# Sample state updates moved in front of the recurrent blocks, and score pages of every second group loaded into partitions 32 to 127

## The chip, the core and the metric

The kernel runs on one core of a Trainium2 chip. The metric is the device time of one execution in microseconds (us), the median of several runs. Engines are named as in the profile: PE (TensorE), DVE (VectorE), ACT (ScalarE), POOL (GpSimd) and SP (SyncE, which only issues transfers here). All engines run their own instruction streams and meet at semaphores.

## The reference, cut to what matters

One step of a two-layer model over a prompt of 512 tokens and, beside it, one new token for each of 8 samples. Everything is float32. Layer 0 has a mixer with two parts, and both occur twice, for the prompt and for the samples:

- an attention with a compressed cache. Each sample attends to 32 pages of 128 past tokens, gathered by a page table from HBM: scores with 8 heads, softmax, and the weighted sum of the values,
- a recurrence (`hgrn2`) with a 128x128 state for each of 4 heads. The prompt starts from zero and goes over 32 chunks of 16 tokens for each head. Each of the 8 samples makes one step from its stored state.

```python
qe = q * jnp.exp(bcum); ke = k * jnp.exp(-bcum); kd = k * jnp.exp(bcum[:, :, -1:] - bcum)
...
def step(S, xs):
    qe_c, kd_c, v_c, dec_c = xs
    o_c = jnp.einsum('btha,bhav->bthv', qe_c, S)
    S = dec_c[..., None] * S + jnp.einsum('btha,bthv->bhav', kd_c, v_c)
    return S, o_c
...
o = o * lax.rsqrt(jnp.mean(o * o, axis=-1, keepdims=True) + RMS_EPS) * g_out.astype(f32)
```

For a sample there is one token, so `S_new = f * S + k v` and `o = q S_new`, then the same norm. The rest of the layers are feed-forward blocks and projections, in which TensorE multiplies without a pause; the change doesn't touch them.

## The kernel before, in words

Everything is written out by hand: each engine has its own stream (`block.sync`, `block.gpsimd`, `block.scalar`, the vector and tensor streams), and in each the same stages follow one another: `ffn("ffn0")`, `ab_in()` (22 weight units), `queries()`, `hgrn()`, `keys()`, `prompts()`, `out_projection("ab_out")`, and the other layers. Weights come through three buffers `raw[0..2]` of 512 KB each, which SP loads in order; ACT and DVE split each into a high and a low part (`prefetch`, lines L250 and L256).

**The page work is spread over the stages by slots.** Numbered slots run from 0 up, and every engine calls `sample_to(end)` at the same places of its stream, which does the page work of all slots below `end`. The ends are set by `after_hgrn`, `after_state`, `after_norm`, `after_kv` and `after_prompt` (written out by hand: 4 slots to each of the 16 recurrent blocks, then 9 slots in the state part, 10 in the norm part, and so on). A *quad* is 4 jobs of 2 pages. Slots 3, 7, 11, ... each do the scores of one quad on PE (`scores`, L1685, 24 matmuls); 20 slots later the same quad's values are done (`values`, L1700); between them is the softmax of a sample, over slots 16 after its first.

Score pages go to `s_raw`, 8 slots for jobs, thus a ring of two quads: SP issues the 8 page loads of quad n+2 when the scores of quad n are done (`load_job`, L466). A score page is 96 partitions of 384 numbers (144 KB). Value pages (128 partitions, 128 KB) go to a ring `v_raw` of the same depth: POOL issues three of each four jobs (`pages_to`), SP the fourth, in between its score loads.

**`hgrn()`** has 16 blocks m (4 heads by 4 token blocks). For each, PE transposes and multiplies (`block_scores`), multiplies keys by values (`outer`, L1784), DVE goes over 8 chunk states one after the other in `s_ring` (L1282, L1285) and PE makes the outputs (L1808, L1814); ACT and DVE take them out of PSUM (L813, L1264). DVE's `sample_queries()` (L1145 to L1162), which lays out the samples' queries `q_s` and waits for the last of them, stands in front of block 0.

Behind block 15 comes **the state part**: k and v of the samples are transposed (L1823), copied (`ks_t` on ACT L821, `v_bd` on DVE L1304), multiplied in three sets (L1843), DVE makes the 32 updates of `st0` to `st7` (L1315), PE the outputs with `q_bd` (L1833), ACT the squares and the norm factors (L825 to L831: a square, `Ln`, `Exp`), DVE scales (L1322, L1325). POOL loads the states (L552): two of them near block 0, two behind block 15, four when the last square is done; it clears `q_bd` (L581) in between, and stores the new states (L589, L593). Then comes **the norm part** (scale, transpose back L1860, gate L1334, split into `m_hi` L838 and `m_lo`), and `keys()`.

Of the kernel before, what the change touches and what calls it, by code (L numbers as in the profile page):

```python
# [37 lines left out]
P = 128  # L38
D_MODEL, SEQ, BATCH_D, D_FF = 1024, 512, 8, 2816
NT = SEQ + BATCH_D  # L40
# [64 lines left out]
def build(nc, dram):  # L105
    ctx = ExitStack()
    with ctx:
# [58 lines left out]
        q_t, = tiles_at(R(0), ("q_t", [P, HEADS, NT]))  # L166
        v_raw = tiles_at(R(8), *[(f"v_raw{i}", [P, JOB, KV_LORA]) for i in range(RING)])
        w_uk, = tiles_at(R(8) + 4 * JOB * KV_LORA * 4, ("w_uk", [NOPE, HEADS, KV_LORA]))
# [4 lines left out]
        st4, st5, st6, st7 = tiles_at(R(28), *[(f"st{i}", [P, BH, P]) for i in range(4, BATCH_D)])  # L173
# [14 lines left out]
        def z_col(u):  # L188
            if u < C_F:
# [4 lines left out]
        kdv0, kdv1, kdv2, att0, att1, att2, v_blk0, v_blk1, s_ring, s_fin, st0, st1, self_row, q_s, own_k, o_lat, decay, p_own_c = tiles_at(  # L194
            work, *[(f"kdv{i}", [P, 2, P]) for i in range(3)], *[(f"att{i}", [P, P]) for i in range(3)],
            *[(f"v_blk{i}", [P, CH_ROW, P]) for i in range(2)], ("s_ring", [P, 2 * CH_BLK, P]), ("s_fin", [P, BH, P]),
            *[(f"st{i}", [P, BH, P]) for i in range(2)], ("self_row", [P, CC * P]), ("q_s", [P, BATCH_D, SK, CG]),
# [4 lines left out]
        st2, st3, v_bd, q_bd = tiles_at(at_blk, ("st2", [P, BH, P]), ("st3", [P, BH, P]), ("v_bd", [P, BATCH_D, P]),  # L202
                                        ("q_bd", [P, BH, BATCH_D * CG]))
        assert 2 * BH * P == 2 * CH_ROW * P and BATCH_D * P + BH * BATCH_D * CG == 2 * CH_BLK * P
        st = [st0, st1, st2, st3, st4, st5, st6, st7]
        kv_pad, ks_t, os_sb = tiles_at(work, ("kv_pad", [P, 2, BH, CG]), ("ks_t", [P, P]), ("os_sb", [P, P]))
# [205 lines left out]

        def after_hgrn(m, part):
            return 4 * m + part + 1

        def after_state(u):
            return 65 + u + 1

        def after_norm(n):
            return 73 + n + 1  # L420

# [30 lines left out]
        Q_S_STEPS = SK + 2  # L452
# [6 lines left out]
        def load_job(eng, kind, k, page_numbers):  # L459
            slots = s_raw if kind == "s" else v_raw  # L460
            if k >= RING:

                eng.wait_ge(S(f"{kind}_done"), k // COLG - RING // COLG + 1)
            rows, lo, width = (SR, 0, S_W) if kind == "s" else (PAGE, SR * S_W, KV_LORA)
            for j in range(JOB):
                eng.dma_start(slots[k % RING][0:rows, j, :],  # L466
                              dram["cache"][bass.ds(page_numbers[j], 1), lo:lo + rows * width].rearrange("a (p w) -> (a p) w", w=width)) \
                    .then_inc(loaded(kind, k), 16)

        def quad_loaded(eng, kind, q):  # L470

            uses = q // 2 + 1
            if kind == "s":
                eng.wait_ge(loaded("s", COLG * q), 16 * JOB * COLG * uses)
# [13 lines left out]
        def _(sp):  # L488
# [8 lines left out]

            sp.dma_start(gain[:], dram["gain"]).then_inc(S("gain_loaded"), 16)
# [39 lines left out]
        def _(pool):  # L538
# [42 lines left out]
            pool.memset(q_bd[:], 0.0).then_inc(S("q_cleared"), 1)  # L581
            pool.wait_ge(S("o_squared"), HG)
            for b in range(HALF_B, BATCH_D):
                state_in(b)
            pool.dma_start(dram["state_p"], s_fin[:]).then_inc(S("s_fin_stored"), 16)
            pages_to(after_state(3))
            pool.wait_ge(S("s_step"), BH * HALF_B)
            for b in range(HALF_B):
                pool.dma_start(dram["state_s"][b], st[b][:]).then_inc(S("st_stored"), 16)  # L589
            pages_to(after_state(7))  # L590
            pool.wait_ge(S("s_step"), BH * BATCH_D)
            for b in range(HALF_B, BATCH_D):
                pool.dma_start(dram["state_s"][b], st[b][:]).then_inc(S("st_stored"), 16)  # L593
# [15 lines left out]
        def _(act):  # L609
# [113 lines left out]
            def queries():  # L723
                n0, g0 = U0["uq"], G0["uq"]
                for h in range(HEADS):
# [12 lines left out]
                    if h in (2, 5, 7):  # L738
                        prefetch(n0 + (2, 5, 7).index(h))
# [46 lines left out]
            def hgrn():  # L786
# [14 lines left out]

                keep(0)
                keep(1)
                for m in range(HG):
# [6 lines left out]
                    sample_to(after_hgrn(m, 1))  # L811
                    act.wait_ge(S("o_mm"), m + 1)
# [5 lines left out]
                act.wait_ge(S("q_cleared"), 1)  # L818
                act.activation(q_bd[:, :, 0:BATCH_D * CG:CG + 1], z_q[:, :, SEQ:NT], ACT.Copy).then_inc(S("q_spread"), 1)
                act.wait_ge(S("kv_turned"), 1)  # L820
                act.activation(ks_t[:], bank[0][:, 0:P], ACT.Copy).then_inc(S("ks_kept"), 1)  # L821
                for u in range(-1, BATCH_D):
                    sample_to(after_state(u))
# [1262 lines left out]
```

## Time and profile before

| | us |
|---|---|
| median of 3 runs (lowest, highest) | 2275.16 (2272.53, 2280.35) |
| the profiled execution: its own time | 2284.63 |
| the profiled execution: its span | 2282.9 |
| PE busy, DVE busy, ACT busy (sum over the span) | 2185.3, 1036.6, 730.8 |
| recurrent blocks 0 to 15, on DVE | 556.95 to 680.34 |
| state part | 680.34 to 719.29 |
| norm part, then `keys()` and `prompts()` | 719.29 to 888.48 |

The last three rows are in us from the span's start. A group of instructions is read by its line number; a busy PE is not PE at its peak, since its matmuls overlap and the clock it is granted changes. The profiled execution is 9.5 us above the median of the runs shown, so differences are formed against its own time and carried over to the median.

### The profile page before, as it was taken

To read this page: it belongs to the slowest core of one execution; us is meant where nothing else is said; L and a number is where in the kernel's file an instruction comes from. 1 tells how busy PE (TensorE), PEld (TensorE's weight loads), DVE (VectorE), ACT (ScalarE), POOL (GpSimd) and SP (SyncE) were. 2 spreads that over 40 slices of the span, in tenths; PEclk is the share of its full clock that TensorE was granted. 3 is DMA by queue.
4 is the path that set the end of the run, shared out by engine and by line. 5 is a ranking of instruction groups with operands and counts; after the bars stand their busy time and mean duration, and the time that the engine had idled before them with its cause. 6 is when DMAs were issued, how large, how long until landed. Compare 5 with 4: busy or idle time off the path is not lost.

```text
span 2282.9 us, 46816 instructions
## 1 busy us (share of the span) xinstructions
PE 2185.3 (96%) x18285; PEld 2072.4 (91%) x18285; DVE 1036.6 (45%) x2002; ACT 730.8 (32%) x1292; POOL 120.2 (5%) x226
## 2 busy tenths in 40 slices
PE   8999999998776789999999999999999999999997
PEld 8999999997443458999999999999999999999997
DVE  5444434366654344544433444443446664444333
ACT  6222223354212333422222232222232233222222
POOL 0000000001234241000000000000000000000000
PEclk9999999998887789999999999999999999999999
DMA  4222223234799872222222222222322222222222
GB/s 162 92 92 92 92 102 100 81 125 147 213 265 279 236 212 93 84 92 92 92 92 100 97 91 91 92 92 92 102 92 92 92 93 92 88 87 91 94 100 75
DMA packets 101037, 261.98 MB, mean 115 GB/s; under 512 B 14385, under 2 KB 49218, under 8 KB 100866
## 3 DMA queue, kind: packets, MB, share of 16 engines
q1 hardware_dynamic: 89746, 228.83, 31.6%
q0 software_dynamic: 11184, 31.69, 4.7%
q8 instruction: 72, 1.18, 0.2%
q14 instruction: 35, 0.29, 0.0%
HBM read 255.29 MB, written 5.16 MB: 114 GB/s over the span
## 4 chain that ended last, share of the span: by engine, by line
PE 61%; DVE 1%; ACT 0%; issue 0%; DVEq 0%; ACTq 0%
PE bank L279 20%; PE bank L278 20%; PE bank L280 20%; PE bank L1929 1%; PE bank L1908 0%; PE bank L303 0%; DVE sb_x L1012 0%; PE bank L1921 0%; PE bank L1700 0%; PE bank L1943 0%; DVE sb_x L373 0%; ACT L312 0%; ACT sb_t L343 0%; DVE sb_h_lo L351 0%; ACT sb_h_hi L338 0%
## 5 line engine op out<-in xcount | busy, mean ns | idle before, releaser
L278 PE MATMUL bank<-sb_h_hi,sb_w_hi 128*128 128x260 f32 x3552 | 1005.9, 283 | 9.8 <-DVE sb_h_lo L1471 8.2
L279 PE MATMUL bank<-sb_h_lo,sb_w_hi 128*128 128x260 f32 x3552 | 1007.1, 284 | 0.0
L280 PE MATMUL bank<-sb_h_hi,sb_w_lo 128*128 128x260 f32 x3552 | 1003.8, 283 | 0.0
L250 ACT ACTIVATE sb_w_hi<-sb_raw 128x1024 fp32r<-128x1024 f32 x339 | 359.7, 1061 | 1260.8 <-PE bank L280 1257.1
L278 PEld LDWEIGHTS bank<-sb_h_hi,sb_w_hi 128*128 128x128 f32 x3552 | 668.5, 188 | 11.5 <-DVE sb_w_lo L256 8.3
L280 PEld LDWEIGHTS bank<-sb_h_hi,sb_w_lo 128*128 128x128 f32 x3552 | 671.4, 189 | 0.0
L279 PEld LDWEIGHTS bank<-sb_h_lo,sb_w_hi 128*128 128x128 f32 x3552 | 668.1, 188 | 0.2
L256 DVE TENSOR_TENSOR sb_w_lo<-sb_raw,sb_w_hi 128x1024 fp32r<-128x1024 f32 x339 | 415.3, 1225 | 382.4 <-ACT sb_w_hi L250 381.6
L279 PE MATMUL bank<-sb_a_lo,sb_w_hi 128*128 128x260 f32 x1408 | 399.1, 283 | 0.0
L278 PE MATMUL bank<-sb_a_hi,sb_w_hi 128*128 128x260 f32 x1408 | 398.7, 283 | 0.0
L280 PE MATMUL bank<-sb_a_hi,sb_w_lo 128*128 128x260 f32 x1408 | 397.7, 282 | 0.0
L280 PEld LDWEIGHTS bank<-sb_a_hi,sb_w_lo 128*128 128x128 f32 x1408 | 265.1, 188 | 0.0
L278 PEld LDWEIGHTS bank<-sb_a_hi,sb_w_hi 128*128 128x128 f32 x1408 | 264.9, 188 | 0.0
L279 PEld LDWEIGHTS bank<-sb_a_lo,sb_w_hi 128*128 128x128 f32 x1408 | 264.5, 188 | 0.0
L980 DVE TENSOR_TENSOR sb_t<-bank,sb_t 128x260 f32<-128x260 f32 x176 | 75.3, 429 | 261.1 <-PE bank L280 258.3
L972 DVE TENSOR_TENSOR sb_t<-bank,sb_r 128x260 f32<-128x260 f32 x176 | 74.4, 425 | 221.3 <-PE bank L280 200.7
L466 POOL DMA_DIRECT2D sb_v_raw<-in_cache x192 | 103.8, 541 | 195.0 <-PE bank L1700 176.2
L1685 PE MATMUL bank<-sb_s_raw,sb_q_s 96*32 96x256 f32 x768 | 60.1, 449 | 16.0 <-DMA sb_s_raw<-in_cache 8.8
L278 PE MATMUL bank<-sb_m_hi,sb_w_hi 128*128 128x260 f32 x256 | 73.2, 286 | 0.8 <-DVE sb_m_lo L1454 0.8
L279 PE MATMUL bank<-sb_m_lo,sb_w_hi 128*128 128x260 f32 x256 | 73.2, 286 | 0.0
L280 PE MATMUL bank<-sb_m_hi,sb_w_lo 128*128 128x260 f32 x256 | 73.0, 285 | 0.0
L985 DVE TENSOR_TENSOR sb_a_lo<-sb_t,sb_a_hi 128x260 f32 (+1 forms) x176 | 67.1, 423 | 0.0
(279 smaller groups left out, 1556.3 us busy)
## 6 DMA issues: line engine op xcount, KB each, us to landing
sb_raw<-in_w SPq DMA_DIRECT2D x339, 512.0 KB, 3.5
sb_s_raw<-in_cache SPq DMA_DIRECT2D x256, 144.0 KB, 4.7
sb_v_raw<-in_cache POOLq DMA_DIRECT2D x192, 128.0 KB, 5.3
sb_v_raw<-in_cache SPq DMA_DIRECT2D x64, 128.0 KB, 5.8
sb_x<-in_x SPq DMA_DIRECT2D x4, 520.0 KB, 6.2
out_y<-sb_x SPq DMA_DIRECT2D x8, 260.0 KB, 2.3
sb_st<-in_state POOLq DMA_DIRECT2D x8, 256.0 KB, 8.2
out_state_s<-sb_st POOLq DMA_DIRECT2D x8, 256.0 KB, 5.7
```

The lines of the kernel that those rows point to most:

```text
L250: nc.scalar.activation(w_hi[slot][:], raw[slot][:], ACT.Copy).then_inc(S("w_hi_done"), 1)
L256: nc.vector.tensor_tensor(w_lo[slot][:], raw[slot][:], w_hi[slot][:], ALU.subtract).then_inc(S("w_lo_done"), 1)
L278: nc.tensor.matmul(out, wh, xh, start=first and c == 0, stop=False)
L279: nc.tensor.matmul(out, wh, xl, start=False, stop=False)
L280: mm = nc.tensor.matmul(out, wl, xh, start=False, stop=last and c == chunks - 1)
L466: eng.dma_start(slots[k % RING][0:rows, j, :], dram["cache"][bass.ds(page_numbers[j], 1), lo:lo + rows * width].rearrange("a (p w) -> (a p ...
L972: dve.tensor_tensor(t1[:, half[hf]], pair(g, hf), r[:, half[hf]], ALU.mult) \
L980: dve.tensor_tensor(t3[:, half[hf]], pair(g + 1, hf), t2[:, half[hf]], ALU.mult) \
L985: dve.tensor_tensor(a_lo[:, ff, half[hf]], t3[:, half[hf]], a_hi[:, ff, half[hf]], ALU.subtract) \
L1685: last = mm(out, q_s[0:SR, i, c, :], s_raw[(COLG * n + j) % RING][0:SR, :, c * P:(c + 1) * P], start=q % 2 == 0 and c == 0, stop=q % 2 == ...
L1929: last = mm(bank[3][:, b * P:(b + 1) * P], v_t[:, k, vals], prob_t[:, tri(b) + k, :], start=k == 0, stop=k == b)
```

## The change

- The state part moves from behind block 15 to in front of block 0. The slots keep their order and number: `after_state(u)` is now `u + 2`, `after_hgrn` starts 9 later, the norm part's slots shift, and the slots of the norm part are handed out head by head.
- The samples' state outputs are normed on their own at the front (`norm_factors`, a `Ln` and an `Exp`), the prompt's 16 blocks behind block 15 (another `Ln` and `Exp`).
- All 8 states are loaded by POOL at once, when `ab_in()` is done. They now lie where the value ring `v_raw` lies, so POOL and SP start the value pages when the new states have been stored (`st_stored`).
- The parts of `sample_queries()` that need no queries (`own_rows`), and the padding of k and v (`state_rows`), go into `ab_in()`, units 20 and 21.
- The third of the weight splits of `queries()` goes to block 3. SP loads that stream's last weight unit before the pages (`n_cache - 1`) behind all pages instead.
- Score pages of odd quads: each page comes in two pieces, its rows 32 to 95 into partitions 32 to 95, and its rows 0 to 31 into partitions 96 to 127 (4 loads for each job instead of 2). POOL clears partitions 0 to 31 of these four slots once, `q_s` gets a copy of its rows 0 to 31 in rows 96 to 127, and the scores of odd quads contract over 128 rows instead of 96.

```diff
         q_t, = tiles_at(R(0), ("q_t", [P, HEADS, NT]))
+        st = tiles_at(R(8), *[(f"st{b}", [P, BH, P]) for b in range(BATCH_D)])
         v_raw = tiles_at(R(8), *[(f"v_raw{i}", [P, JOB, KV_LORA]) for i in range(RING)])
...
+        def after_state(u):
+            return u + 2
         def after_hgrn(m, part):
-            return 4 * m + part + 1
-        def after_state(u):
-            return 65 + u + 1
+            return 9 + 4 * m + part + 1
...
+            pieces = ((0, 0, rows),) if kind == "v" or k // COLG % 2 == 0 else ((LOW, LOW, SR - LOW), (SR, 0, LOW))
             for j in range(JOB):
-                eng.dma_start(slots[k % RING][0:rows, j, :],
-                              dram["cache"][bass.ds(page_numbers[j], 1), lo:lo + rows * width].rearrange("a (p w) -> (a p) w", w=width)) \
-                    .then_inc(loaded(kind, k), 16)
+                for to, row, count in pieces:
+                    first = lo + row * width
+                    eng.dma_start(slots[k % RING][to:to + count, j, :],
+                                  dram["cache"][bass.ds(page_numbers[j], 1), first:first + count * width].rearrange("a (p w) -> (a p) w", w=width)) \
+                        .then_inc(loaded(kind, k), 16)
...
-            stream(n_mid, n_cache)
+            stream(n_mid, n_cache - 3)
+            load(n_cache - 3)
+            load(n_cache - 2)
...
-                    if k - LAG == RING - 1:
-                        sp.wait_ge(S("q_lat_mm"), 1)
+                    if k - LAG == COLG - 1:
+                        sp.wait_ge(S("st_stored"), 16 * BATCH_D)
                     load_job(sp, "v", k - LAG, page_numbers(sp, k - LAG, 1)[0])
+            load(n_cache - 1)
```

POOL's stream, from the load of `w_uk` on:

```diff
-            pages_to(LAG - 4)
-            pool.wait_ge(S("ckv_stored"), 16)
-            pool.wait_ge(S("q_s_ready"), Q_S_STEPS)
-            state_in(0)
-            state_in(1)
+            for b in range(BATCH_D):
+                state_in(b)
+            pool.wait_ge(S("half_done"), 2 * U0["ukv"])
+            for i in range(COLG, RING):
+                pool.memset(s_raw[i][0:LOW], 0.0).then_inc(S("s_cleared"), 1)
             pool.wait_ge(S("q_lat_mm"), 1)
+            pool.memset(q_bd[:], 0.0).then_inc(S("q_cleared"), 1)
+            pool.wait_ge(S("s_step"), BH * HALF_B)
+            for b in range(HALF_B):
+                pool.dma_start(dram["state_s"][b], st[b][:]).then_inc(S("st_stored"), 16)
+            pool.wait_ge(S("s_step"), BH * BATCH_D)
+            pool.wait_ge(S("os_mm"), 1)
+            for b in range(HALF_B, BATCH_D):
+                pool.dma_start(dram["state_s"][b], st[b][:]).then_inc(S("st_stored"), 16)
+            pool.wait_ge(S("st_stored"), 16 * BATCH_D)
             for m in range(HG):
                 pages_to(after_hgrn(m, 3))
             pool.wait_ge(S("final_kept"), BH)
-            pool.wait_ge(S("o_mm"), HG)
-            state_in(2)
-            state_in(3)
-            pool.memset(q_bd[:], 0.0).then_inc(S("q_cleared"), 1)
-            pool.wait_ge(S("o_squared"), HG)
...
             pool.dma_start(dram["state_p"], s_fin[:]).then_inc(S("s_fin_stored"), 16)
```

DVE's `hgrn()` (the loop of the updates, lines L1307 to L1318, moves as it is), and what goes from `sample_queries()` into `ab_in()`:

```diff
+                    if u == 20:
+                        own_rows()
+                    if u == 21:
+                        state_rows()
...
+                dve.wait_ge(S("kv_turned"), 1)
+                dve.tensor_copy(vs_t[:], V_BANK[:, 0:P]).then_inc(S("vs_kept"), 1)
+                sample_queries()
+                dve.wait_ge(S("q_lat_mm"), 1)
+                dve.wait_ge(S("vs_kept"), 1)
+                dve.tensor_tensor(v_bd[:], vs_t[:].unsqueeze(1).to_broadcast([P, BATCH_D, P]),
+                                  cst[:, C_DIAG:C_DIAG + BATCH_D].unsqueeze(2).to_broadcast([P, BATCH_D, P]), ALU.mult).then_inc(S("v_spread"), 1)
...
                 masked(0)
                 masked(1)
-                sample_queries()
+                dve.wait_ge(S("o_factor"), 1)
+                dve.tensor_scalar(os_sb[:], os_sb[:], o_fac[:, HG:HG + 1], None, ALU.mult).then_inc(S("o_scaled"), 1)
+                dve.wait_ge(S("o_turned_back"), 1)
...
+                dve.tensor_copy(q_s[SR:P, :, :, 0:HEADS], q_s[0:LOW, :, :, 0:HEADS]).then_inc(S("q_s_ready"), 1)
```

ACT's `hgrn()`, and PE's scores:

```diff
                 keep(0)
                 keep(1)
+                act.wait_ge(S("os_kept"), 1)
+                act.activation(os_sq[:], os_sb[:], ACT.Square, accum_out=o_ss[:, HG:HG + 1]).then_inc(S("os_squared"), 1)
+                act.wait_ge(S("os_squared"), 1)
+                norm_factors(slice(HG, HG + 1), 1)
                 for m in range(HG):
...
+                    if m == 3:
+                        prefetch(U0["uq"] + UQ_UNITS - 1)
...
                 squared(HG - 1)
+                act.wait_ge(S("o_squared"), HG)
+                norm_factors(slice(0, HG), 2)
...
-                        last = mm(out, q_s[0:SR, i, c, :], s_raw[(COLG * n + j) % RING][0:SR, :, c * P:(c + 1) * P],
+                        last = mm(out, q_s[rows, i, c, :], s_raw[(COLG * n + j) % RING][rows, :, c * P:(c + 1) * P],
```

## Rows read from the trace of the kernel before

**Rows 1.** The page: the span, and the issues of the state loads (KB each, us to landing)

```profile
span 2282.9 us, 46816 instructions
...
sb_st<-in_state POOLq DMA_DIRECT2D x8, 256.0 KB, 8.2
```

**Rows 2.** Windows by stage: length, busy of PE, PEld, DVE, ACT, POOL, clock, DMA share, GB/s

```profile
556.95:581.35 24.40, 19.51 (x204) 10.16 (x204) 16.28 (x48) 3.61 (x13) 4.29 (x8) 0.77 0.61 186
581.35:680.34 98.99, 75.45 (x820) 41.72 (x818) 55.51 (x173) 23.03 (x72) 32.28 (x60) 0.90 0.97 247
680.34:719.29 38.95, 25.41 (x216) 11.24 (x216) 14.13 (x49) 7.33 (x17) 17.49 (x32) 0.68 0.99 272
719.29:730.91 11.62, 10.59 (x105) 6.09 (x105) 7.21 (x17) 2.31 (x6) 4.35 (x9) 0.74 0.93 288
```

**Rows 3.** Waits, 680.3 to 719.3 us: total, times, longest

```profile
DVE sb_st L1315 <- DMA sb_st<-in_state: 11.1, 1, 11.1
ACT sb_q_bd L819 <- POOL sb_q_bd L581: 10.1, 1, 10.1
...
PE bank L1843 <- ACT sb_ks_t L821: 6.3, 1, 6.3
```

**Rows 4.** DVE's and PE's timeline at the front of `hgrn()`

```profile
549.79 0.33 PE L1772 MATMUL bank<-sb_cst,sb_kd 128*128 128x128 f32 x1
...
556.55 0.52 DVE L1162 COPY sb_q_s<-bank 96x64 f32<-96x64 f32 x3
556.95 0.27 DVE L1282 COPY sb_s_ring<-bank 128x128 f32<-128x128 f32 x1
```

**Rows 5.** Timeline of the state part on PE, DVE and ACT

```profile
684.92 0.44 PE L1823 MATMUL bank<-sb_cst,sb_kv_pad 128*128 128x128 f32 x2
...
685.39 1.23 DVE L1304 TENSOR_TENSOR sb_v_bd<-bank,sb_cst 128x1024 f32<-128x1024 f32 x1 [4.13 <-PE bank L1823]
...
691.69 2.08 PE L1843 MATMUL bank<-sb_v_bd,sb_ks_t 32*128 32x512 f32 x6 [6.33 <-ACT sb_ks_t L821]
...
698.78 3.19 DVE L1315 SCALAR_TENSOR_TENSOR sb_st<-sb_st,sb_f_s,bank 128x128 f32<-128x128 f32 x12 [11.12 <-DMA sb_st<-in_state]
...
711.06 1.10 DVE L1315 SCALAR_TENSOR_TENSOR sb_st<-sb_st,sb_f_s,bank 128x128 f32<-128x128 f32 x4
...
715.18 0.28 ACT L825 ACTIVATE sb_os_sb<-bank 128x128 f32<-128x128 f32 x1 [15.22 <-PE bank L1833]
...
718.83 0.22 ACT L831 ACTIVATE sb_o_fac<-sb_o_fac 128x17 f32<-128x17 f32 x1
```

**Rows 6.** ACT: the first table load of the softmax; the page: a weight's split on DVE

```profile
589.11 1.28 ACT L768 ACT_TABLE_LOAD   x1
...
L256 DVE TENSOR_TENSOR sb_w_lo<-sb_raw,sb_w_hi 128x1024 fp32r<-128x1024 f32 x339 | 415.3, 1225 | 382.4 <-ACT sb_w_hi L250 381.6
```

**Rows 7.** SP's timeline: a quad's score pages, its value job, the next quad

```profile
616.82 3.86 SPq L466 DMA_DIRECT2D sb_s_raw<-in_cache  x8
621.38 0.90 SPq L466 DMA_DIRECT2D sb_v_raw<-in_cache  x2
623.26 5.34 SPq L466 DMA_DIRECT2D sb_s_raw<-in_cache  x8
```

**Rows 8.** Score pages from issue to landing, all in the first row, 620 to 685 in the second

```profile
DMA to landing us min/median/max: 2.1/4.7/12.7
...
DMA to landing us min/median/max: 5.0/7.9/11.2
```

**Rows 9.** PE's timeline: the first values, and the scores that end the norm part

```profile
600.56 1.22 PE L1700 MATMUL bank<-sb_v_raw,sb_p_t 128*32 128x256 f32 x16
...
733.89 1.50 PE L1685 MATMUL bank<-sb_s_raw,sb_q_s 96*32 96x256 f32 x24 [2.02 <-DMA sb_s_raw<-in_cache]
```

**Rows 10.** Waits of PE for pages, 550 to 870 us: total, times, longest

```profile
PE bank L1685 <- DMA sb_s_raw<-in_cache: 8.8, 5, 3.9
...
PE bank L1700 <- DMA sb_v_raw<-in_cache: 1.7, 2, 1.2
```

More of the change, by code:

```diff
@@ L201, in build @@
         at_blk = work + 3 * 2 * P * 4 + 3 * P * 4
[L202 to L206, printed above, removed]
+        v_bd, q_bd = tiles_at(at_blk + 2 * BH * P * 4, ("v_bd", [P, BATCH_D, P]), ("q_bd", [P, BH, BATCH_D * CG]))
+        w_uk, = tiles_at(at_blk + 2 * BH * P * 4, ("w_uk", [NOPE, HEADS, KV_LORA]))
+        assert BH * P == CH_ROW * P and BATCH_D * P + BH * BATCH_D * CG == 2 * CH_BLK * P == HEADS * KV_LORA
+        ks_t, vs_t = tiles_at(at_r, ("ks_t", [P, P]), ("vs_t", [P, P]))
         k_t, prob = tiles_at(work, ("k_t", [P, HEADS, SEQ]), ("prob", [P, 10, P]))
@@ L451, in build @@
         HB = HEADS * BATCH_D
-        Q_S_STEPS = SK + 2
+        Q_S_STEPS = SK + 3
+        LOW = P - SR
         GATES = 6
@@ L816, in hgrn @@
                 squared(HG - 1)
[L818 to L823, printed above, removed]
[L824 to L832 removed]
+                act.wait_ge(S("o_squared"), HG)
+                norm_factors(slice(0, HG), 2)
                 for h in range(BH):
[L834 removed]
+                    sample_to(after_norm(h))
                 act.wait_ge(S("o_turned_back"), BH + 1)
@@ L1852, in hgrn @@
                 outputs(1)
-                for h in range(-1, BH):
-                    pe.wait_ge(S("o_scaled"), h + 2)
-                    if h < 0:
-                        last = nc.tensor.transpose(O_BANK[:, 0:P], os_sb[:], ident)
-                    else:
-                        for b in range(BLOCKS):
-                            last = nc.tensor.transpose(bank[h][:, b * P:(b + 1) * P], kd[:, h, o_block(h, b)], ident)
+                block_scores(0)
+                block_scores(1)
@@ new lines, in hgrn @@
+                pe.wait_ge(S("os_kept"), 1)
+                outer(0)
+                pe.wait_ge(S("o_scaled"), 1)
+                nc.tensor.transpose(O_BANK[:, 0:P], os_sb[:], ident).then_inc(S("o_turned_back"), 1)
+                for m in range(HG):
+                    h, b = divmod(m, BLOCKS)
+                    if m + 2 < HG:
+                        block_scores(m + 2)
+                    sample_to(after_hgrn(m, 0))
+                    if m + 1 < HG:
+                        outer(m + 1)
+                    else:
+                        pe.wait_ge(S("state_step"), CH_BLK * HG)
+                    sample_to(after_hgrn(m, 1))
+                    if m:
+                        pe.wait_ge(S("o_kept"), m)
+                    else:
+                        pe.wait_ge(S("o_step"), 1)
+                    mm(O_BANK[:, 0:2 * P], att[m % 3][:], kdv[m % 3][:, 1:2, :].to_broadcast([P, 2, P]), start=True, stop=False)
+                    for odd in range(2):
+                        for j in range(COLG):
+                            c = 2 * j + odd
+                            if b or c:
+                                cols = slice(b * P + j * CG, b * P + (j + 1) * CG)
+                                last = mm(O_BANK[CG * j:CG * (j + 1), odd * P:(odd + 1) * P], qe[:, h, cols],
+                                          s_ring[:, (CH_BLK * m + c) % (2 * CH_BLK), :], start=False, stop=odd == 1)
+                    last.then_inc(S("o_mm"), 1)
+                    sample_to(after_hgrn(m, 3))
@@ L1861, in hgrn @@
+                pe.wait_ge(S("kv_kept"), HG)
+                pe.wait_ge(S("att_masked"), HG)
+                for h in range(BH):
+                    pe.wait_ge(S("o_scaled"), h + 2)
+                    for b in range(BLOCKS):
+                        last = nc.tensor.transpose(bank[h][:, b * P:(b + 1) * P], kd[:, h, o_block(h, b)], ident)
                     last.then_inc(S("o_turned_back"), 1)
-                    sample_to(after_norm(1 if h < 0 else 2 + h))
+                    sample_to(after_norm(h))
```

189 lines of the change are left out of this document (83 added, 106 removed).

## The prediction

> **What bounds the kernel now.** I went from the page to the windows by stage, then to the waits and timelines of the part that the change moves. Outside `hgrn()`, `keys()` and `prompts()` TensorE multiplies weights without a pause, and the change leaves that alone. So the question is how long the stretch from 549.8 us, when PE turns to `hgrn()` [rows 4], to `ab_out` becomes. In the windows [rows 2] no engine is full there: in blocks 4 to 15 PE is busy 75.5 of 99.0 us and DVE 55.5; in the state part DVE is busy 14.1 of 39.0 us and PE 25.4, with PE's clock granted at 0.68 of full, so partly at the lower of its two levels (1.2 and 2.4 GHz). It is a chain of waits from engine to engine. Beside it the DMA share stands at 0.97 to 0.99: the page transfers have little room.
>
> **The state part is mostly waiting** [rows 3]: DVE stands 11.1 us before its first update for states whose loads POOL issued only behind block 15, and ACT stands 10.1 us for POOL's clearing of `q_bd`, with the copy `ks_t` queued behind it, so PE waits 6.3 us. At the front all of this can be ready: POOL issues the eight loads of 256 KB [rows 1] at about 528 us, and they took a median of 8.2 us to land (11.1 us of wait as the upper bound), against a first use near 555. Should they be late, DVE's wait comes back, up to 11.1 us.
>
> **The front part, step by step, from 549.8 us.** Transposes of k and v 0.4, v's copy 0.3 (the width of the 0.28 copy at 715.18). Four copies of queries 0.2 + 0.5, and the new one into partitions 96 to 127, which no row shows: as many numbers in each partition as the three of 0.52 together, so 0.2 to 0.5, I take 0.3. `v_bd` 1.2, the first set of L1843 2.1 [rows 4, 5]. That is 5.0: 554.8. The 32 updates with the scores of two quads beside them ran from 698.78 to 712.16, 13.4 us [rows 5]; of that 1.6 was softmax work on DVE, which at slots 0 to 8 doesn't exist yet: 11.8, giving 566.6. Last outputs and `os_sb` 715.46 - 712.16 = 3.3: 569.9. Square, `Ln`, `Exp`, with two table loads, 719.05 - 715.46 = 3.6 [rows 5], and in front of them the copies of blocks 0 and 1 (`keep`), about 1.0: 574.5. DVE waits for this factor before its first block, then scales, waits for a transpose and gates, 1.1: 575.6. DVE's first chunk state was at 556.95 [rows 4], so the blocks start **18.7 us later**. This already contains `sample_queries()`, on either side. Its other copies and clearings (2.8 us) go to unit 20 of `ab_in()`, where DVE stands idle beside PE's 5.8 us for a unit; uncovered they would cost 2.8. The padding (0.6) stands before the first query drain and may cost 0 to 0.6; I take 0.
>
> **The blocks.** Blocks 0 to 3 took 24.40 us, 6.1 each; blocks 4 to 15, with softmax and then values in their slots, took 98.99, 8.25 each [rows 2]. With nine slots gone before block 0, the softmax begins at slot 16 in block 1 rather than in block 4, 2.25 blocks earlier: 2.25 x 2.15 = **+4.8**. The weight split in block 3 costs DVE 1.2 [rows 6] in a chain that DVE is part of: +1.2 (0 if it falls into a wait, 2.3 with ACT's half). The 1.28 us table load before the first `Exp` of the softmax [rows 6] goes, since the front has loaded that table: -1.3. The split's removal from the end of `queries()` is worth nothing: PE's last latent queries set 549.8, not DVE.
>
> **Behind block 15.** The norm factors of the prompt are now exposed: square, `Ln` and `Exp` with both table loads, **+3.6** [rows 5]. The whole state part, 38.95 us [rows 2], is gone from here. Slots are as far on as before when the norm part begins, so `keys()` and `prompts()` have the same work. Sum of the chain: 18.7 + 4.8 + 1.2 - 1.3 + 3.6 - 38.95 = **-11.9 us**.
>
> **The pages.** The bytes stay. What changes is SP's queue. Eight score loads take 3.86 us, 0.506 from one to the next, and the next two parts start 0.7 us and 0.9 us after; the value job is 0.90 [rows 7]. So an even quad holds SP for 6.4 us and an odd one, with 16 loads, for 15 x 0.506 + 0.32 + 2.5 = 10.4. A pair is 16.8 us of issuing against 16.5 us of blocks: SP goes from two thirds busy to full. And the last piece of an odd quad is issued 7.9 us after the release of its slots, not 3.9. The release comes two blocks before the use, so 16.5 - 1.5 (the scores) - 7.9 leaves 7.1 us for the landing, where before 11.1 were left. In 620 to 685 us the landing took 5.0 / 7.9 / 11.2 (shortest, median, longest), over the whole kernel a median of 4.7 [rows 8]. Queued loads explain the difference: at twice the issues for the same bytes fewer bytes stand in the queue, and I expect 5 to 7. So in the blocks I take no loss beyond SP's 0.3 us a pair, 2 us, against the waits for pages there that may go. In the norm part, four quads come within some 20 us: the last already waited 2.0 us [rows 9], SP can now deliver one each 8.4 us, and the state part is no longer there to let the ring fill up: +1 to +5, I take 2. With half of the 2 us in the blocks given back by fewer waits, the pages cost +3 (bounds: -10.5, which is every wait of PE for a page [rows 10], and the rival below). SP no longer loads the last weight unit before the pages, which lets them start some 4 us sooner; the slots are filled ahead of use either way: 0. Value loads begin only when the states are stored, which takes some 8 us behind the last outputs (estimated from the 8.2 of their loads), so near 578 us. The first values stood at 600.6 us [rows 9] and move to about 597; two quads are issued by then: 0.
>
> The Trainium skill has a rule that speaks against two pieces: "SBUF — State Buffer", section "Can I just issue two DMAs to hit both halves?", says no, the two serialize, measured at only +6% over one. By it the split brings nothing and only its issues stay, which is the sum as I have it. The trace before has no split page to compare.
>
> **The sum.** -11.9 + 3 = **-9 us**. Against its own 2284.6 us that is 2275.6 for a profiled execution, 2266.2 against the median of 2275.2. What a measurement can tell from no change is about 0.3%, 6.8 us.
>
> **The rivals.**
>
> *A. The gain is eaten by the pages* (chance 0.24). The DMA share of 0.97 in the blocks says that they may already run at the pace of the transfers, and PE's waits for pages are few only because chain and transfers have the same pace. Then what the chain gains comes back as waits in the norm part and `prompts()`. The same bytes in 12 us less, at the 272 GB/s of the state part instead of 247, would fit, which speaks against it. Its time: 9 us less 5 to 9, 2266 to 2275, I say 2271.
>
> *B. Balanced partitions make the pages faster* (0.14). In `s_raw` all pages lay in partitions 0 to 95. If transfers are limited where they enter these partitions, spreading them shortens every landing, and the 10.5 us of PE's waits for pages [rows 10] go: 2275.2 - 11.9 - 10.5 + 2 = 2255. For it: landings at 7.9 in the busy stretch where the shortest took 2.1 [rows 8]. Against: 272 GB/s were reached with the old layout. The Trainium skill, "SBUF — State Buffer", "Door 1: The DMA port swizzle", has partitions 0 to 63 on one half of the ports and 64 to 127 on the other; by it the old pages gave one half two thirds of their bytes, the new ones in turn give each half the same. No row here shows a port.
>
> *C. SP's queue and the landing of odd quads set the pace: slower* (0.17). Place: SP's 16 issues for an odd quad, then the landing, then the scores on PE, in blocks 2 to 15. A pair of blocks lasts at least 7.9 + landing + 1.5. It decides where the landing passes 7.1 us, and eats 9 us over 7 pairs from 8.4 us on; the median of now is 7.9. At 10 us, between that median and the longest of 11.2 [rows 8], a pair takes 19.4 instead of 16.5: 7 x 2.9 = 20, so 2275.2 - 9 + 20 = 2286.
>
> *D. The change doesn't do what it says* (0.03): the states arrive late at the front or the odd quads' loads start as late as before, so that the 11.1 us wait returns: 2277.
>
> **How the numbers follow.** My forecast of 2266 has 0.42, spread over 2260 to 2272 by the bounds above (front 18 to 22, norm 1 to 5). A 0.24, B 0.14, C 0.17, D 0.03. Faster by over 6.8 us (below 2268.4): 0.34 of the forecast's 0.42, 0.06 of A, all of B: 0.54. Slower (above 2282.0): most of C: 0.14. The rest, 0.32, is the same. The range of 2254 to 2281 takes in forecast, A, D and most of B, and leaves out C's upper part.
>
> **What would show it.** Right: the updates L1315 start near 555 us with no wait for `sb_st`; the first chunk state (L1282) near 576; block 15 ends near 704; the norm part's scaling (the four L1325 of now) starts near 708 instead of 719.3; PE's waits for `sb_s_raw` sum to under 15 us. SP's odd quads show 16 issues in 7.9 us. Wrong: a first chunk state later than 580 (the front was costed too low); blocks slower than 8.5 us each with PE or DVE waiting for pages (C); a landing median above 8 us (C) or below 4.5 with blocks at 7.9 or less (B); a norm part longer than 17 us instead of 11.6 [rows 2] (A).

## The result, and the profile after

The changed kernel takes **2316.6 us** (median of 4 runs, 2316.2 to 2317.6) where the kernel before took 2275.5 in the same session: a ratio of 1.0179 [1.0161, 1.0197], 41 us **slower**. The forecast was 2266 with a range of 2254 to 2281, so even the range failed, and the rival on the slow side (2286) stopped far short.

The page of the changed kernel, its first part and the score pages: where they are multiplied (to set beside [rows 10]), how many packets all DMA queues moved, and how long whole pages and the larger pieces took to land (the smaller ones: 2.7 us too).

```profile
span 2315.9 us, 47204 instructions
...
PE 2191.7 (95%) x18285; PEld 2073.9 (90%) x18285; DVE 1036.8 (45%) x2004; ACT 733.7 (32%) x1295; POOL 122.4 (5%) x230
...
DMA packets 103088, 262.01 MB, mean 113 GB/s; under 512 B 16433, under 2 KB 51266, under 8 KB 102914
...
L1722 PE MATMUL bank<-sb_s_raw,sb_q_s 96*32 96x256 f32 (+1 forms) x768 | 62.2, 463 | 26.6 <-DMA sb_s_raw<-in_cache 21.6
...
sb_s_raw<-in_cache SPq DMA_DIRECT2D x128, 144.0 KB, 3.3
sb_s_raw<-in_cache SPq DMA_DIRECT2D x128, 96.0 KB, 2.7
```

The engines do the same work as before: DVE is busy 0.2 us longer, ACT 2.9, PE 6.4. The span is 33.0 us longer, so most of that is waiting. And a page takes less long to land than in [rows 8], although PE waits for pages more.

**The front came as forecast.** The timeline of the changed kernel from the first query copy to the first chunk state:

```profile
550.75 1.15 DVE L1189 COPY sb_q_s<-sb_q_t 32x64 f32<-32x64 f32 x1
...
552.49 0.25 DVE L1197 COPY sb_q_s<-sb_q_s 32x192 f32<-32x192 f32 x1
...
556.19 3.19 DVE L1307 SCALAR_TENSOR_TENSOR sb_st<-sb_st,sb_f_s,bank 128x128 f32<-128x128 f32 x12 [2.19 <-PE bank L1851]
...
577.13 0.28 DVE L1343 COPY sb_s_ring<-bank 128x128 f32<-128x128 f32 x1
```

The updates find the states loaded (DVE waits for PE's products, not for a load), and the first chunk state, forecast at 575.6, stands at 577.1. One copy took 1.15 us where I had 0.2.

**Behind it nothing did.** The last `z_q` copy of the blocks, on ACT, is at 730.83 us; forecast was an end near 704. So the blocks last 153.7 us, where they had 123.0 before (556.95 to 679.94, by the same two instructions). The norm part's scaling starts at 737.49 us, forecast at 708. By windows:

```profile
core 0: us, PE busy (x) PEld busy (x) DVE busy (x) ACT busy (x) POOL busy (x), PEclk, DMA share, GB/s
601.00:723.00 122.00, 86.49 (x851) 44.10 (x844) 56.82 (x174) 23.95 (x72) 35.39 (x66) 0.84 0.75 212
723.00:740.00 17.00, 8.67 (x80) 5.41 (x79) 6.63 (x17) 5.41 (x12) 6.98 (x13) 0.84 0.79 240
740.00:780.00 40.00, 29.86 (x258) 17.21 (x260) 9.88 (x24) 15.17 (x24) 12.87 (x24) 0.80 0.79 234
780.00:820.00 40.00, 28.52 (x208) 15.67 (x204) 15.61 (x42) 9.65 (x26) 12.88 (x24) 0.76 0.74 224
```

The DMA share is the thing to see. It was 0.97 in blocks 4 to 15 of before [rows 2] and is 0.75 here, and 0.74 to 0.79 behind the blocks: the transfers have room now. Either SP doesn't issue fast enough, or the blocks don't ask for pages fast enough. SP's own timeline, here for one pair of quads and the start of the next:

```profile
610.86 11.07 SPq L471 DMA_DIRECT2D sb_s_raw<-in_cache  x16
622.65 0.90 SPq L471 DMA_DIRECT2D sb_v_raw<-in_cache  x2
624.28 3.86 SPq L471 DMA_DIRECT2D sb_s_raw<-in_cache  x8
628.83 0.90 SPq L471 DMA_DIRECT2D sb_v_raw<-in_cache  x2
630.47 11.55 SPq L471 DMA_DIRECT2D sb_s_raw<-in_cache  x16
```

An even quad costs SP what it did before [rows 7], 3.86 us. An odd quad costs 10.7 to 11.9 us (11.1 on average), not the 7.9 of the forecast, and this pair of quads 19.6 us, not 16.8. From 600 to 860 us SP waits 3.0 us in all:

```profile
SPq L471 <- PE bank L1722: 3.0, 2, 2.6
```

In the kernel before it stood 91 us of the same stretch waiting for PE to release slots:

```profile
SPq L466 <- PE bank L1685: 67.2, 21, 9.6
SPq L466 <- PE bank L1700: 24.0, 5, 9.5
```

Odd quads begin at 610.86 and, twelve pairs later, at 856.72: 20.5 us a pair on average.

Two waits grew, in the waits of 548 to 900 us (us in total, times, longest):

```profile
PE bank L1821 <- DVE sb_s_ring L1346: 40.4, 15, 3.9
DVE sb_mx_h L1202 <- PE bank L1722: 38.9, 13, 4.8
```

The same two before:

```profile
PE bank L1784 <- DVE sb_s_ring L1285: 19.2, 10, 4.5
...
DVE sb_mx_h L1168 <- PE bank L1685: 6.7, 7, 2.2
```

Neither names a page. So there were two suspects: SP's issuing, and something in the blocks that the move brought.

### The profile page after: what moved, and what is told of

The parts are those of the page before. It is cut to its first block, busy times and chain, and to the rows that moved or that the text cites. A ratio compares the mean times of both kernels' runs of the same rounds, so it can differ in the third digit from the quotient of the medians.

```text
span 2315.9 us, 47204 instructions
## 1 busy us (share of the span) xinstructions
PE 2191.7 (95%) x18285; PEld 2073.9 (90%) x18285; DVE 1036.8 (45%) x2004; ACT 733.7 (32%) x1295; POOL 122.4 (5%) x230
## 2 busy tenths in 40 slices
DMA packets 103088, 262.01 MB, mean 113 GB/s; under 512 B 16433, under 2 KB 51266, under 8 KB 102914
## 4 chain that ended last, share of the span: by engine, by line
PE 60%; DVE 1%; issue 1%; ACT 0%; DMA 0%; DVEq 0%; POOLq 0%; ACTq 0%; POOL 0%
PE bank L277 20%; PE bank L276 20%; PE bank L278 19%; PE bank L1969 0%; DMA sb_v_raw<-in_cache 0%; PE bank L301 0%; DVE sb_x L1026 0%; PE bank L1983 0%; DVE sb_x L371 0%; ACT L310 0%; PE bank L1961 0%; PE bank L1737 0%; ACT sb_t L341 0%; DVE sb_h_lo L349 0%; ACT sb_h_hi L336 0%
## 5 line engine op out<-in xcount | busy, mean ns | idle before, releaser
L1722 PE MATMUL bank<-sb_s_raw,sb_q_s 96*32 96x256 f32 (+1 forms) x768 | 62.2, 463 | 26.6 <-DMA sb_s_raw<-in_cache 21.6
L1722 PEld LDWEIGHTS bank<-sb_s_raw,sb_q_s 96*32 96x32 f32 (+1 forms) x768 | 29.3, 134 | 51.2 <-issue 21.3
```

Source lines behind the costliest of these rows:

```text
L1722: last = mm(out, q_s[rows, i, c, :], s_raw[(COLG * n + j) % RING][rows, :, c * P:(c + 1) * P], start=q % 2 == 0 and c == 0, stop=q % 2 == ...
```

## The experiments

Each ran beside the kernel before, on the same chip in the same session; ratios are to it. There were four sessions on three chips, with the kernel before at 2278.2 to 2280.3 us, so runs of different sessions are compared by their ratios.

| Run | What it is | median us | ratio [95%] |
|---|---|---|---|
| e1_move_only | the move, pages whole | 2295.9 | 1.0077 [1.0062, 1.0093] |
| e2_split_only | before, pages in two | 2319.6 | 1.0176 [1.0156, 1.0196] |
| e3_split_low | after, pieces in partitions 0 to 95 | 2312.3 | 1.0142 [1.0121, 1.0163] |
| e4_whole_high | after, odd quads whole in 32 to 127 | 2297.3 | 1.0088 [1.0067, 1.0110] |
| f1_move_phase0 | e1, slots one part earlier | **2271.5** | **0.9958 [0.9943, 0.9972]** |
| f2_before_phase1 | before, slots one part later | 2297.2 | 1.0069 [1.0052, 1.0086] |
| f3_move_phase2 | e1, slots one part later | 2293.4 | 1.0065 [1.0048, 1.0082] |
| f5_after_phase0 | after, slots one part earlier | 2315.3 | 1.0157 [1.0140, 1.0174] |
| g1_after_phase0_values_pool | f5, POOL issues all values | 2287.1 | 1.0048 [1.0033, 1.0063] |
| g2_move_phase0_values_pool | f1, POOL issues all values | 2275.0 | 0.9990 [0.9974, 1.0005] |
| g3_whole_high_phase0 | f1, odd quads whole in 32 to 127 | 2271.6 | 0.9973 [0.9963, 0.9984] |
| h1_column_halves_phase0 | f1, odd quads in two column halves | 2282.7 | 1.0010 [0.9993, 1.0027] |

### The two parts of the change alone

Move only: the changed kernel with

```diff
-            pieces = ((0, 0, rows),) if kind == "v" or k // COLG % 2 == 0 else ((LOW, LOW, SR - LOW), (SR, 0, LOW))
+            pieces = ((0, 0, rows),)
```

the semaphore count and the rows of the multiplication to match, and POOL's clearing of partitions 0 to 31 gone.

> The changed kernel with the page part undone: every score page again comes in one transfer into partitions 0 to 95, the rest of the change stays (the copy of query rows to partitions 96 to 127 stays too). T1, the issuing of score pages on SP costs the time: the move alone brings what its chain brought, about 9 to 12 us, so 2264 to 2268, with block 15 ending near 704 and the norm part's scaling near 708; SP's pair of quads back near 12.8 us of issuing. T2, the partitions cost the time: the same 2264 to 2268. T3, the move itself costs the time (softmax earlier, value loads late, blocks slower): above 2280, up to the 2316 of the changed kernel.

Measured: 1.0077. T1 and T2 are wrong as they stand: **the move by itself loses 17.5 us (0.77%) instead of winning 9**. The page part is the rest, 1.0%; by the spans of the two profiles, 2293.5 and 2315.9 us, it is 22 us. Its blocks are as slow as the changed kernel's (575.46 to 728.66 us, 153.2) while SP waits 85 us of 600 to 860 for PE, so T3 is alive for the blocks. The two waits are there in full, and the page waits aren't (the changed kernel had 21.6 us of them):

```profile
PE bank L1817 <- DVE sb_s_ring L1344: 40.1, 15, 3.9
DVE sb_mx_h L1200 <- PE bank L1718: 33.0, 10, 4.6
...
PE bank L1718 <- DMA sb_s_raw<-in_cache: 6.3, 2, 4.0
```

Its windows say what the DMA share can tell:

```profile
601.00:723.00 122.00, 86.48 (x848) 44.15 (x848) 56.85 (x174) 24.27 (x74) 37.04 (x69) 0.85 0.79 217
...
780.00:820.00 40.00, 32.22 (x226) 17.75 (x225) 16.38 (x47) 10.86 (x28) 14.11 (x27) 0.71 0.94 258
```

In the blocks it is nearly as low as in the changed kernel (0.79 against 0.75) though SP has time to spare: there the low share only says that the blocks are slow. Behind the blocks it is 0.94 against 0.74, and that difference is SP's.

Split only: the kernel before with the `pieces` of the change, the copy of query rows and the clearing, and nothing moved.

> The kernel before with the page part alone: odd quads in two pieces into partitions 32 to 127, state updates still behind the blocks. T1: SP is the bound of a pair of quads from the first page on, as in the changed kernel (20.2 us a pair), and the last value load comes at about the same time as there, so 2308 to 2320 although the state part stands where it stood; PE's waits for the scores' releases on SP fall from 103 us to under 40. T3: the page part is harmless, 2270 to 2280. If the move's gain of some 9 us were additive, it would be 2325.

Measured: 1.0176, the loss of the whole change. In the blocks odd quads again hold SP for 11.1 to 11.8 us. T1 as forecast. The losses of the two parts, 0.8% and 1.8%, together make 1.8% and not 2.6%: the smaller hides behind the larger.

### Is it the place of the pieces?

```diff
-            pieces = ((0, 0, rows),) if kind == "v" or k // COLG % 2 == 0 else ((LOW, LOW, SR - LOW), (SR, 0, LOW))
+            pieces = ((0, 0, rows),) if kind == "v" or k // COLG % 2 == 0 else ((0, 0, 2 * LOW), (2 * LOW, 2 * LOW, LOW))
```

> The changed kernel with the odd quads' pages still in two pieces (64 rows, then 32), but at the old partitions 0 to 63 and 64 to 95, and 96 rows in the multiplication. T1, number of issues: odd quads still take 16 issues and about 11 us, a pair 20 us, time 2310 to 2318. T2, what costs is where the pieces land (partitions 32 and 96): issues of pieces fall to the 0.5 us spacing of whole pages, a pair 16.8 us, 2265 to 2280.

Measured: 1.0142, and on SP:

```profile
609.45 10.81 SPq L471 DMA_DIRECT2D sb_s_raw<-in_cache  x16
```

Two pieces at the old partitions are nearly as dear: 10.1 to 11.1 us a quad, on average 0.6 less than in the changed kernel, and 0.4% less in the time. The other half of that question is one piece at the new partitions:

```diff
-            pieces = ((0, 0, rows),) if kind == "v" or k // COLG % 2 == 0 else ((LOW, LOW, SR - LOW), (SR, 0, LOW))
+            pieces = ((0 if kind == "v" or k // COLG % 2 == 0 else LOW, 0, rows),)
```

> The changed kernel with the odd quads' pages in one transfer each, of 96 rows in order into partitions 32 to 127; the rows of the queries are not put into that order, so the scores of the odd quads are multiplied with the wrong query rows (the work is the same). T1: 8 issues of 0.5 us spacing for both kinds of quad, a pair 12.8 us of issuing, time 2260 to 2268 like the move alone. T2, partitions above 96 or a start at 32 cost issue or landing time: near 2316, or landings longer than the 3 to 8 us of the whole pages in partitions 0 to 95. T4, spread partitions speed the landing: below the move alone by more than 3 us.

Measured: 1.0088, level with e1; every quad takes 3.9 to 5.0 us again. T2 and T4 are out here, and T1 stands: what costs is that a page comes in two pieces. But the 2260 to 2268 of T1 failed with e1's, from the same cause.

### What makes the blocks slow? A shift by one part

The timeline of the changed kernel shows one block; PE and DVE only:

```profile
668.79 1.00 PE L1889 MATMUL bank<-sb_s_ring,sb_z_q 128*32 128x128 f32 x16
...
669.62 1.47 PE L1722 MATMUL bank<-sb_s_raw,sb_q_s 128*32 128x256 f32 x24
...
671.16 0.69 DVE L1202 TENSOR_REDUCE sb_mx_h<-bank 128x1 f32<-128x512 f32 x1 [4.54 <-PE bank L1722]
...
672.22 1.50 DVE L1346 SCALAR_TENSOR_TENSOR sb_s_ring<-sb_s_ring,sb_decay,bank 128x128 f32<-128x128 f32 x4
...
673.89 1.56 DVE L1346 SCALAR_TENSOR_TENSOR sb_s_ring<-sb_s_ring,sb_decay,bank 128x128 f32<-128x128 f32 x4
...
675.60 0.70 PE L1821 MATMUL bank<-sb_v_blk,sb_kdv 64*128 64x512 f32 x2 [3.05 <-DVE sb_s_ring L1346]
```

DVE needs nothing new for its first four state updates; PE had the products ready at 667.7. But in DVE's order the maximum over a sample's scores stands in front of them, and PE multiplies these scores only behind the block's outputs. DVE stands 4.54 us, then has both groups of four still to do, and PE stands 3.05 us for them. The cause lies in a number: the slots stood at `4m + part + 1` in block m before, and at `9 + 4m + part + 1` now, because the state part took its nine. Nine is two blocks **and one part**. The experiment puts eight there:

```diff
         def after_hgrn(m, part):
-            return 9 + 4 * m + part + 1
+            return 8 + 4 * m + part + 1
```

> The move alone (pages whole, as in the run e1_move_only) with one number changed: the sample slots stand at 8 + 4m + part in block m, not at 9 + 4m + part, so that they fall on the same parts of a block as in the kernel before. T5, a matter of phase: with 9, DVE's maximum over a sample's scores comes in front of a block's first group of state updates and waits there 4.5 us for scores that PE multiplies only behind the block's outputs; with 8 the full blocks fall from 10.1 to about 8.3 us, ten blocks are worth 15 to 19 us, time 2275 to 2283 (2295.9 less 13 to 20). T6, blocks are 10 us because softmax and values overlap with more of them, wherever the slots fall: 2293 to 2298, blocks stay at 10.

Measured: 2271.5, ratio 0.9958: **faster than both kernels**, and by more than T5 said. Block stage 575.11 to 702.88 us, 127.8. The scaling of the norm part, 719.29 in the kernel before:

```profile
707.65 0.69 DVE L1362 TENSOR_TENSOR sb_kd<-sb_kd,sb_o_fac 128x512 f32<-128x512 f32 x1 [3.62 <-ACT sb_o_fac L822]
```

And a like stretch of f1's timeline, with the order turned round: a first group of updates runs before the scores, and only the second comes behind the maximum:

```profile
646.52 1.49 DVE L1344 SCALAR_TENSOR_TENSOR sb_s_ring<-sb_s_ring,sb_decay,bank 128x128 f32<-128x128 f32 x4
...
648.12 2.40 PE L1718 MATMUL bank<-sb_s_raw,sb_q_s 96*32 96x256 f32 x24
...
650.59 0.69 DVE L1200 TENSOR_REDUCE sb_mx_h<-bank 128x1 f32<-128x512 f32 x1 [1.61 <-PE bank L1718]
...
651.64 1.55 DVE L1344 SCALAR_TENSOR_TENSOR sb_s_ring<-sb_s_ring,sb_decay,bank 128x128 f32<-128x128 f32 x4
```

Its waits:

```profile
PE bank L1817 <- DVE sb_s_ring L1344: 20.8, 13, 2.6
...
PE bank L1718 <- DMA sb_s_raw<-in_cache: 13.8, 9, 3.9
```

If this is the cause, one part of shift must spoil the kernel before as well, where nothing is moved:

```diff
         def after_hgrn(m, part):
-            return 4 * m + part + 1
+            return 1 + 4 * m + part + 1
```

> The kernel before with one number changed: the sample slots of the blocks one part later (1 + 4m + part), everything else as it was. T5 (phase): the blocks with values become 10 us instead of 8.2, so 12 to 18 us slower, 2287 to 2295. T6: 2273 to 2280, no change.

Measured: 1.0069, 16 us by the ratio and within T5's 12 to 18 (its 2287 to 2295 is missed by 2 us, since the kernel before itself stood at 2280.3 here). Its blocks take 152.6 us (557.11 to 709.70) instead of 123.0, and the waits are those of the changed kernel:

```profile
PE bank L1784 <- DVE sb_s_ring L1285: 41.0, 14, 4.5
DVE sb_mx_h L1168 <- PE bank L1685: 34.0, 10, 6.0
```

Of the 29.6 us that its blocks lose, about half comes back later. A maximum is taken over each of the 16 half samples: the ninth, behind the blocks, is 24 us late (737.4 against 713.0), the last is 14 us late (855.4 against 841.4).

One part later instead:

> As f1 but with 10 + 4m + part, one part later than in the changed kernel. T5: the maximum then stands at another part again; if what matters is only that it doesn't stand in front of the first updates, blocks fall below 9.5 us and the time to 2275 to 2290; T6: 2293 to 2298.

Measured: 1.0065. The blocks last 154.8 us (575.33 to 730.12). The expectation took it that with two parts of shift the maximum no longer stands in front of a block's first updates. It still does; only PE multiplies the scores earlier (664.07 us in the block shown), ahead of the block's outputs (L1879, L1885 from 666.37) instead of behind them:

```profile
665.64 0.69 DVE L1200 TENSOR_REDUCE sb_mx_h<-bank 128x1 f32<-128x512 f32 x1 [1.96 <-PE bank L1718]
...
666.70 1.50 DVE L1344 SCALAR_TENSOR_TENSOR sb_s_ring<-sb_s_ring,sb_decay,bank 128x128 f32<-128x128 f32 x4
```

DVE stands 25.1 us for the maxima (33.0 in e1, 10.7 in f1), and PE stands 36.7 us for `s_ring` (40.1 and 20.8). So this run does not speak against the cause: the order on DVE is the bad one again. How its loss divides between the shorter waits for the maxima and the rest is not shown, and the fourth offset of the four was not run.

### What does the better phase bring the changed kernel?

> The whole changed kernel, its pages in two pieces, with the sample slots at 8 + 4m + part. T1 and T5 together: the blocks can't use the better phase, since SP needs 20.2 us for a pair of quads, just what two blocks of 10.1 take, so the time stays at 2312 to 2318. If SP were not a bound of its own it would fall by the same 13 to 20 us as the move alone, to about 2300.

Measured: 1.0157. Its block chain is repaired (PE waits 18.7 us for `s_ring`, as in f1), and it helps nothing: PE waits for pages instead.

```profile
PE bank L1722 <- DMA sb_s_raw<-in_cache: 41.7, 14, 8.0
```

So in the changed kernel SP's pace is the bound and the slow blocks hide behind it (they cost it 0.2%). That they hide is chance: two blocks of 10 us are just a pair of quads on SP.

### SP's queue, relieved and loaded

In g1 and g2 POOL issues the fourth value job of each quad, which was SP's:

```diff
-                    numbers = page_numbers(pool, COLG * quads[0], 3)
-                    for j in range(3):
+                    numbers = page_numbers(pool, COLG * quads[0], 4)
+                    for j in range(4):
```

> The whole changed kernel with pages in two pieces, the slots at 8 + 4m + part, and the one value job of every quad that SP issued now issued by POOL with the other three. T1, SP's issuing of score pages is the bound: without its two value jobs of 1.64 us each a pair of quads falls from 20.0 to 16.6 us, about the pace of the blocks, so most of the 43 us between f5_after_phase0 (2315) and f1_move_phase0 (2271.5) comes back: 2273 to 2290. If the pieces cost by something other than SP's queue (memory, landing, PE), it stays at 2305 or above.

Measured: 1.0048, so by the ratios 1.1% or 25 us faster than f5 with the same pieces in the same places. T1 as forecast. SP is still close to its limit: from 600 to 860 us it waits 13.4 us, of which 1.2 fall into this stretch:

```profile
619.99 70.22 SPq L471 DMA_DIRECT2D sb_s_raw<-in_cache  x98
```

98 issues in 70.2 us is 17.2 us for the 24 of a pair (16.9 without the wait), and the rest of the loss against f1 is there: PE's waits for score pages are 34.6 us against 13.8.

> The best so far, f1_move_phase0 (2271.5), with all value jobs issued by POOL. In f1 SP has 12.8 us of issuing in a pair of quads of about 16.4 us and is no bound: 2268 to 2276. Slower than 2278 only if POOL, which then issues 8 value loads a quad at some 0.6 us, or its queue becomes the limit.

Measured: 2275.0, in the range, and by the ratio (0.9990 against 0.9958) rather worse than f1: an SP that isn't the bound gains nothing from the same relief.

> f1_move_phase0 with the odd quads' pages in one transfer each, into partitions 32 to 127 (as in the run e4_whole_high the query rows are not put into that order, so the odd quads' scores are not the reference's). In f1 the DMA share is 0.99 and the score pages take 8.9 us to land in 620 to 685 us, so here, unlike in e4, transfers are a limit. Rival B, partitions 0 to 95 limit the transfers: landing falls below 7.5 us, time 2258 to 2267. No such limit: within 3 us of f1, 2269 to 2275, with landings of 8 to 9.5 us.

Measured: the median of f1, and by the ratio (0.9973, its interval overlaps f1's) no gain on it. In 620 to 685 us, f1 and then g3:

```profile
sb_s_raw<-in_cache SPq DMA_DIRECT2D x60, 144.0 KB, 8.9
```

```profile
sb_s_raw<-in_cache SPq DMA_DIRECT2D x62, 144.0 KB, 7.4
```

In this stretch the landing is 1.5 us shorter with the odd pages in the upper partitions. That is not shown to come from the partitions: over the whole kernel the same pages land no faster, f1 first and then g3,

```profile
sb_s_raw<-in_cache SPq DMA_DIRECT2D x256, 144.0 KB, 5.3
```

```profile
sb_s_raw<-in_cache SPq DMA_DIRECT2D x256, 144.0 KB, 5.5
```

and from 700 to 860 us they take 4.7 and 5.5 us. PE's waits for score pages are 13.2 us against 13.8. Rival B is worth nothing to this kernel, and its faster landing shows in a part of the stages only.

The last run asks for the price of an issue. It has as many issues as the row pieces and the same bytes, but each names all 96 rows:

```diff
+                for part in range(halves):
+                    cols = slice(part * width // halves, (part + 1) * width // halves)
+                    eng.dma_start(slots[k % RING][0:rows, j, cols], page[:, cols]).then_inc(loaded(kind, k), 16)
```

> As f1_move_phase0 (slots at 8 + 4m + part, partitions 0 to 95), but each page of an odd quad comes as two transfers of all 96 rows and half of each row, so 16 issues of 72 KB. It tests the price of an issue: with two row pieces SP took 10.4 to 11.8 us for 16 issues, where I had forecast 7.9. If it was the row pieces that were dear and 16 issues of the full form cost 7.9 us, a pair is 16.9 us of issuing: 2274 to 2288. If any second issue for a page costs as much as the pieces did, a pair stays at 20 us: 2308 to 2316.

Measured: 2282.7 (1.0010), no different from the kernel before, and by the ratios 0.5% or 12 us slower than f1, its own base. SP:

```profile
624.20 8.56 SPq L472 DMA_DIRECT2D sb_s_raw<-in_cache  x16
...
642.04 7.86 SPq L472 DMA_DIRECT2D sb_s_raw<-in_cache  x16
```

The best odd quads take exactly the 7.9 us of the forecast, others up to 9.5; the average is 8.3, against 11.1 for row pieces. These halves make **more** packets (115376 on the page) than the row pieces (103088), and are issued faster. So the extra 3 us of an odd quad don't come from the number of issues, of bytes or of packets, but from the form of the row pieces, 64 and 32 rows instead of 96 (their place was worth 0.6 us in e3).

The trace says where the extra time lies. These are SP's DMA instructions in one odd quad each, shortest/median/longest in ns; first the changed kernel's at 610.86 us, then h1's at 642.04:

```profile
L471 SPq DMA_DIRECT2D sb_s_raw<-in_cache x16: 331/487/566, 610.9 to 621.5; - x16
```

```profile
L472 SPq DMA_DIRECT2D sb_s_raw<-in_cache x16: 317/317/337, 642.0 to 649.6; - x16
```

The DMA instruction itself is 0.17 us longer, 2.7 us for 16; the register instructions between take 29 to 51 ns each in both. A whole page's instruction takes 317 ns as well. What in the row pieces makes the instruction longer no run shows.

## Why the prediction was wrong, point by point

**The front: right.** 575.6 forecast, 577.1 measured (575.1 in f1). Terms inside it were off and in part cancel: the first query copy was 1.15 us, not 0.2, and the updates began at 556.2, not 554.8.

**"8.25 each ... 2.25 blocks earlier: 2.25 x 2.15 = +4.8": the first step that failed.** I read the nine slots as an amount, 2.25 blocks of softmax, and let the quarter be a quarter of a cost. It is a shift of the order within each block. The forecast for the block stage was 128.4 us (575.6 to 704): f1 has 127.8, and the changed kernel 153.7. The step's sum was right for eight slots (its terms were not measured singly) and 25 us off for nine. The code had this written out, and [rows 2] could not warn of it, since a mean over blocks holds one phase only.

**Behind block 15: right once the phase is.** f1's scaling starts 11.6 us earlier than in the kernel before (707.65 against 719.29), where the chain's sum said 11.9; of this 8.8 us arrive in the time (2280.3 to 2271.5).

**"An odd one, with 16 loads, for 15 x 0.506": the second, and the one that set the result.** It took the spacing of whole pages for that of row pieces. Measured are 10.7 to 11.9 us for 16 issues instead of 7.9, so a pair of 20.5 us on average (the shortest 19.6) instead of 16.8. The forecast stood 0.3 us over the 16.5 us of two blocks; the real pair stands 3 to 4 us over and has nowhere to hide. Even near its own price of an issue the +3 was too small: h1, whose odd quads take 8.3 us, loses 12 us to f1 where the sum has 3, and PE waits 20.8 us there for score pages against 13.8. "SP goes from two thirds busy to full" was the sentence to stop at. A queue that is full has no margin for an error in the price of one issue, so its bound should have been set on either side as for every unseen operation: at 0.6 or 0.7 us an issue, a pair is 18 to 20 us.

**"In the norm part ... I take 2."** I charged pages only where quads come close together. A queue that is the bound charges every pair: it is at 20.5 us over all twelve. Behind the blocks, from the tenth maximum at 747.2 us to the last at 852.0, the move alone needs 104.7 us for six half samples, the changed kernel 120.8 (751.8 to 872.5). That is where 16 us of the page part's 22 are lost.

**The rivals.** C had the place, SP's 16 issues and the odd quads, and the sign. Its price was hung on the landing, "from 8.4 us on"; the landing fell, to 2.7 to 3.3 us where the forecast had 5 to 7. A long landing and a starved queue are opposites, and my test of "a landing median above 8 (C)" would have cleared the guilty one. Its 7 pairs should have been all that SP issues, 12 and more. A has a part in it: half of what f2's blocks lose comes back in the later stages. B is out for the time (e4, g3). D did not happen.

**The rule weighed.** Two pieces brought no gain in time: with them in any form run here (row pieces in either place, column halves) the kernel is slower than with whole pages. The Trainium skill, "SBUF — State Buffer", section "Can I just issue two DMAs to hit both halves?", says that the two serialize. By that rule the split brings nothing; no run here measures the transfers alone, and what agrees is that no split run gained. That "only its issues stay" is safe only once the issues are priced in their own form. Whole pages with every second quad in the other partitions landed in 7.4 us instead of 8.9 in one stretch and in 5.5 instead of 4.7 in a later one. The section "Door 1: The DMA port swizzle" of that page in the Trainium skill gives a reason why balanced partitions might help; no run here shows a port, and here they bought no time.

## What to carry to other kernels

When a hand-written interleave is moved, ask what its new offset is modulo the period of what it is woven into; a shift by one part cost 0.7% to 1.2% here (16 to 27 us) where nothing else was the bound. When a change takes a queue from two thirds to full, price each of its issues in the form they will have, and look for a queue that never waits; a fallen DMA share alone is no sign of it, since slow blocks lower it as well. And undo both parts of a change, singly and together: here undoing the pieces brought 1.0%, undoing the shift 0.2%, and both 2.2%.

## What was not expected of the hardware

On SP 16 issues of row pieces (64 and 32 rows, 96 and 48 KB) took 10.1 to 12.7 us, 16 of 96 rows and half the columns 7.9 to 9.5, and 8 of whole pages 3.9 when nothing delayed them: mostly 0.7, 0.5 and 0.5 us each. The difference lies in the DMA instruction itself: medians of 0.49 and 0.32 us in the two quads shown. And from 620 to 685 us whole pages of 144 KB landed in 3.6 us in e1, where quads are issued 10 us apart, and in 7.9 in the kernel before [rows 8], where they come every 8 to 9 us.
